# Two output tiles per weight unit, and two PSUM banks in turn, in the output projection of a decoder step

## The reference

```
h      = rms_norm(x, norm_g)
z      = h @ w_in                      # feeds four branches and the merge gates
y_n    = branch_n(z)                   # retention, gated delta, short convolution, pooling; width 512 each
merged = sum_n sigmoid(gate_n) * (y_n @ w_branch[n])
x      = x + merged @ w_out            # the output projection, 2048 x 2048
```

## Time and profile before

| what | value |
|---|---|
| three runs | 2049.70, 2051.76, 2053.64 us (median 2051.76) |
| profiled execution, first to last instruction | 2049.6 us |
| PE busy / weight loads busy | 1992.3 / 1976.0 us |
| DVE busy | 1346.1 us |
| ACT busy | 1113.6 us |
| POOL busy | 186.5 us |
| mean granted TensorE clock | 0.993 |

### The profile page before, as it was taken

The page is one execution under the profiler, slowest core; times in us unless marked ns, Lnnn a source line. Parts: engine busy times, 40 slices in busy tenths (PEclk is TensorE's granted clock), DMA queues, the critical chain, the costliest instruction groups (busy, mean ns, idle before and its releaser), DMA issues.

```text
span 2049.6 us, 50596 instructions
## 1 busy us (share of the span) xinstructions
PE 1992.3 (97%) x16294; PEld 1976.0 (96%) x16294; DVE 1346.1 (66%) x2608; ACT 1113.6 (54%) x2045; POOL 186.5 (9%) x345
## 2 busy tenths in 40 slices
PE   6999999999999999999999999999999999999996
PEld 6999999999999999999999999999999999999996
DVE  7887566755656556666678766676565656566666
ACT  5556556645455555555555655655464645455554
POOL 2111110110101010000011210001010100100000
PEclk9999999999999999999999999999999999999998
DMA  6655555555554545665656555655555555566664
GB/s 209 190 175 172 157 181 162 184 160 156 154 172 135 176 140 167 188 180 180 184 172 184 171 173 155 190 164 175 165 162 160 162 155 149 160 175 179 178 184 161
DMA packets 183252, 348.13 MB, mean 170 GB/s; under 512 B 20592, under 2 KB 20720, under 8 KB 182992
## 3 DMA queue, kind: packets, MB, share of 16 engines
q1 hardware_dynamic: 177552, 326.45, 53.4%
q0 software_dynamic: 5568, 19.80, 3.0%
HBM read 333.61 MB, written 12.56 MB: 169 GB/s over the span
## 4 chain that ended last, share of the span: by engine, by line
PE 90%; DVE 4%; issue 3%; ACT 2%; DMA 1%; DVEq 0%; ACTq 0%; SPq 0%
PE acc L1301 27%; PE acc L1302 27%; PE acc L1303 26%; DMA raw<-w_stream 1%; PE side L1514 1%; PE side L1488 1%; DVE wlo L829 1%; PE side L1512 1%; PE side L1505 1%; ACT whi L540 1%; PE side L1396 1%; PE side L1495 1%; PE side L1402 1%; PE side L1358 1%; DVE act_lo L841 0%
## 5 line engine op out<-in xcount | busy, mean ns | idle before, releaser
L829 DVE TENSOR_TENSOR wlo<-raw,whi 128x512 fp32r<-128x512 f32 x1219 | 828.3, 694 | 488.4 <-ACT whi L540 481.4
L540 ACT ACTIVATE whi<-raw 128x512 fp32r<-128x512 f32 x1219 | 751.5, 628 | 643.7 <-PE acc L1303 553.9
L1301 PE MATMUL acc<-act_hi,whi 128*128 128x264 f32 x3328 | 972.6, 292 | 40.1 <-issue 19.6
L1303 PE MATMUL acc<-act_hi,wlo 128*128 128x264 f32 x3328 | 947.8, 285 | 0.0
L1302 PE MATMUL acc<-act_lo,whi 128*128 128x264 f32 x3328 | 947.2, 285 | 0.0
L1301 PEld LDWEIGHTS acc<-act_hi,whi 128*128 128x128 f32 x3328 | 631.8, 190 | 48.2 <-issue 35.9
L1302 PEld LDWEIGHTS acc<-act_lo,whi 128*128 128x128 f32 x3328 | 632.8, 190 | 0.9
L1303 PEld LDWEIGHTS acc<-act_hi,wlo 128*128 128x128 f32 x3328 | 629.4, 189 | 0.0
L1301 PE MATMUL acc<-y_hi,whi 128*128 128x264 f32 x1536 | 439.9, 286 | 0.0
L1302 PE MATMUL acc<-y_lo,whi 128*128 128x264 f32 x1536 | 435.4, 283 | 0.0
L1303 PE MATMUL acc<-y_hi,wlo 128*128 128x264 f32 x1536 | 434.8, 283 | 0.0
(11 more groups left out here) (267 smaller groups left out, 1438.2 us busy)
## 6 DMA issues: line engine op xcount, KB each, us to landing
raw<-w_stream SPq DMA_DIRECT2D x1220, 256.0 KB, 2.8
state<-ret_in POOLq DMA_DIRECT2D x8, 512.0 KB, 5.5
s_ret<-state POOLq DMA_DIRECT2D x8, 512.0 KB, 4.6
state<-gdn_in POOLq DMA_DIRECT2D x8, 512.0 KB, 5.4
s_gdn<-state POOLq DMA_DIRECT2D x8, 512.0 KB, 6.1
x<-x_in SPq DMA_DIRECT2D x4, 528.0 KB, 6.5
y_out<-wide SPq DMA_DIRECT2D x4, 396.0 KB, 2.8
con<-consts SPq DMA_DIRECT2D x1, 1582.0 KB, 11.8
```

What stands on the lines that cost most here:

```text
L540: sc.activation(whi[:, s, :], raw[:, s, :], ACT.Copy).then_inc(hi_ready, 1)
L829: ve.tensor_tensor(wlo[:, s, :], raw[:, s, :], whi[:, s, :].bitcast(F32), ALU.subtract).then_inc(lo_ready, 1)
L1301: mm(acc[bank][:, 0:N], w_h, hi[:, k0 + k, :], start=first and k == 0, stop=False)
L1303: op = mm(acc[bank][:, 0:N], w_l, hi[:, k0 + k, :], start=False, stop=last and k == UK - 1)
```

## The change

A unit of the output projection now holds two k-tiles of two neighbouring output tiles instead of four k-tiles of one. PE takes a pair of output tiles through eight units. Within a unit every matmul writes the other bank than the one ahead of it. The pair is finished at once, so DVE and ACT handle two tiles together, every eight units. Stream length, unit size and the number of matmuls are unchanged. The last turn of the ACT and DVE loops is written out after the loop.

```diff
-                with pe.Fori(0, BT) as h:
-                    unit = streamer(l, OFF_O, h, TURN)
-                    blocks(unit, 0, TURN, pe.snap(l * BANK_USES + BK_O + h), y_hi, y_lo, ready=mlo_ready)
+                def pair(ub, j, bank, k0, first, last):
+
+                    pe.wait_ge(lo_ready, ub + j + 1 + RING)
+                    s = j % RING
+                    for k in range(2):
+                        cols = [slice((2 * k + b) * P, (2 * k + b + 1) * P) for b in range(2)]
+                        for b in range(2):
+                            mm(acc[bank + b][:, 0:N], whi[:, s, cols[b]], y_hi[:, k0 + k, :], start=first and k == 0, stop=False)
+                        for b in range(2):
+                            mm(acc[bank + b][:, 0:N], whi[:, s, cols[b]], y_lo[:, k0 + k, :], start=False, stop=False)
+                        for b in range(2):
+                            op = mm(acc[bank + b][:, 0:N], wlo[:, s, cols[b]], y_hi[:, k0 + k, :], start=False,
+                                    stop=last and k == 1)
+                    op.then_inc(unit_used, 1)
+
+                with pe.Fori(0, BT) as h:
+                    ub = pe.snap(l * UNITS + OFF_O + h * TURN)
+                    free = pe.snap(l * BANK_USES + BK_O + h)
+                    for i in (0, 2):
+                        pe.wait_ge(bank_free[i], free + BF)
+                        pe.wait_ge(bank_free[i + 1], free + BF)
+                        for u in range(2 * UB):
+                            if i == 0:
+                                pe.wait_ge(mlo_ready, l * UB * UK + 2 * (u + 1))
+                            pair(ub, i * UB + u, i, 2 * u, u == 0, u == 2 * UB - 1)
```

DVE (ACT follows the same order, with its square and `act_hi` where DVE has `x_added` and `x_lo`, and waits for `x_updated` of each tile there):

```diff
-                with dve.Fori(0, BT) as h:
+                def out_turn(h, last):
                     ub, split = splitter(l, OFF_O, h, TURN)
-                    for i in range(4):
-                        split(4 * i + 3, 4 * i + 7)
-                        k = dve.snap(h * 4 + i)
-                        dve.wait_ge(unit_used, ub + RING + UB * (i + 1))
-                        ve.tensor_tensor(tile_of(x, k), tile_of(x, k), acc[i][:, 0:N], ALU.add).then_inc(bank_free[i], 1)
-                        dve.wait_ge(bank_free[i], l * BANK_USES + BK_O + h + 1 + BF)
-                        dve.sem_inc(x_updated, 1)
-                        x_added(i % 2, l * KT + h * 4 + i)
-                        x_lo(l + 1, k, (l + 1) * KT + h * 4 + i)
+                    for a in (0, 8):
+                        split(a + 5, a + 11)
+                        dve.wait_ge(unit_used, ub + RING + a + 2 * UB)
+                        for t in (a // 4, a // 4 + 1):
+                            k = dve.snap(h * 4 + t)
+                            ve.tensor_tensor(tile_of(x, k), tile_of(x, k), acc[t][:, 0:N], ALU.add).then_inc(bank_free[t], 1)
+                            dve.wait_ge(bank_free[t], l * BANK_USES + BK_O + h + 1 + BF)
+                            dve.sem_inc(x_updated, 1)
+                        for i in range(2):
+                            if not (last and a):
+                                split(a + 11 + i, a + 12 + i)
+                            t = a // 4 + i
+                            x_added(t % 2, l * KT + h * 4 + t)
+                            x_lo(l + 1, dve.snap(h * 4 + t), (l + 1) * KT + h * 4 + t)
+
+                ub, split = splitter(l, OFF_O, 0, TURN)
+                split(3, 5)
+                with dve.Fori(0, BT - 1) as h:
+                    out_turn(h, False)
+                out_turn(BT - 1, True)
...
-    for m in range(KT):
-        parts += [units(w_out, m * P)]
+    for m in range(0, KT, 2):
+        two = w_out[:, :, m * P:(m + 2) * P].reshape(DEPTH, KT // 2, 2, P, 2 * P)
+        parts += [two.transpose(0, 1, 3, 2, 4).reshape(DEPTH, KT // 2, P, UC)]
```

More of the change, by code:

```diff
@@ L801, in _ @@
                     merged_hi(k)
-                with act.Fori(0, BT) as h:
+                def out_turn(h, last):
                     ub, split = splitter(l, OFF_O, h, TURN)
-                    for i in range(4):
-                        split(4 * i + 3, 4 * i + 7)
[L808 to L811, removed]
+                    for a in (0, 8):
[4 more added lines that the diff above has]
+                            t = a // 4 + i
+                            k = act.snap(h * 4 + t)
+                            act.wait_ge(x_updated, l * KT + h * 4 + t + 1)
+                            x_square(k, t % 2, l * KT + h * 4 + t)
+                            x_hi(l + 1, k)
+                ub, split = splitter(l, OFF_O, 0, TURN)
+                split(3, 5)
+                with act.Fori(0, BT - 1) as h:
+                    out_turn(h, False)
+                out_turn(BT - 1, True)
             for k in range(FINAL_DVE, KT):
```

## The result

| | before | after |
|---|---|---|
| median of 20 runs each | 2051.61 us | 2054.59 us |
| profiled execution, first to last instruction | 2049.6 us | 2053.6 us |
| first projection, first to last matmul start | 92.68 us | 93.90 us |
| second projection | 92.68 us | 93.90 us |

The ratio is 1.0015, 95% interval 1.0009 to 1.0021: 3.1 us slower (1.8 to 4.3). The forecast was 2053.4, with a range of 2048.5 to 2059.

The account below looks back on a forecast made before the run. The prediction took the distance between PE's matmul starts to bound the projections. It added 0 for the loop, 0.65 us for the first layer's end and 0.93 for the kernel's end: +1.6, 2053.4 us, range 2048.5 to 2059.

Parts of the forecast that it names:

- PE's matmul distance bounds the stage; DVE, ACT and the transfers hide.: Output projections: the distance between matmul starts sets the stage; work of the other engines and transfers adds 0 within the loop.
- the 2.1 us that the prediction named: Slack expected in the loop between DVE's split of unit 11's weights after a pair and PE's need for them.
- A bank change costs 0.: Output projections: switching PSUM bank at every matmul costs nothing, argued from 15 bank changes in the old projection.
- Hence the distance stays 0.12083.: Both projections: 1536 matmul distances stay at 0.12083 us each, adding 0 to the time.
- its own sign ("I am wrong if the distance is not 0.1208"): Stated test of failure: a projection matmul distance other than 0.1208 us, or PE waiting for `wlo` within the stage.
- its first rival, a cost of bank changes: Projections: each bank change costs up to 8 ns, giving 2065.7 us; it decides from 1.6 ns a matmul; chance 0.10.
- The bounds (-7.7 to +12.3 us): Both projections: possible effect of bank changes, -5 to +8 ns per matmul times 1536; 0 was taken.
- Nothing of the 10.8 ns above 264 columns at 2.4 GHz belongs to the bank.: Projection matmuls: the 10.8 ns beyond 0.1100 us is no same-bank penalty; the rival that it is had chance 0.07.
- Added waits on PE are free.: Projection turns: 8 waits on `mlo_ready` instead of 4, all already met, cost 0.
- End of the first layer, +0.65 us.: After the first layer's last matmul, ACT's handling of two tiles delays PE's fourth unit of the second layer by 0.65 us.
- The end, +0.93 us.: After the kernel's last matmul, DVE's second sum comes 0.94 us later, so the square root starts 0.93 us later.
- The clock stays.: Projections: PE stays at 2.4 GHz; the rival of a falling clock gave 2130 us, chance 0.02.

Follow-up runs that it names:

- e1: Changed kernel, but both tiles of a pair accumulate in one bank, so no bank change at every matmul: first projection 93.90 us.
- e3: Changed kernel with old units and old order of weights and activations, evacuation in pairs, banks written in turn by every matmul: first projection 92.68 us.
- e4: Changed kernel with old units, old order and one bank for 48 matmuls, keeping evacuation in pairs: projection 92.68 us, whole 1.0004 of the kernel before.
- e5: Changed kernel's units, but per k-tile three matmuls of one output tile, then three of the other: projection 93.90 us, whole 1.0026 of the kernel before.
- e6: Changed kernel with the y_hi and y_lo tiles padded to 272 columns apart instead of 264: projection 93.12 us.
- e7: Changed kernel, but every projection matmul reads the first tile of y_hi or y_lo (products not the reference's): projection 92.04 us.
- e2: Changed kernel's units, but six matmuls of one output tile, then six of the other, k-tiles in old order: projection 92.58 us, whole 1.0007 of the kernel before.
- e10: Changed kernel reading tiles 0 and 8, then 1, then 4 within each turn: tile 4's units took 1480 or 1481 ns in turns one and three, 1440 or 1441 otherwise.

## Why the prediction was right, and where its steps were off

- *PE's matmul distance bounds the stage; DVE, ACT and the transfers hide.* Right: PE waits for nothing in either projection, after as before. ACT's two waits for a transfer (2.8 us together) did not reach PE: the split of every unit was done 0.8 us or more before PE began it, and from the sixth unit on the 2.1 us that the prediction named.
- *A bank change costs 0.* Right, and now shown: e1 against the changed kernel and e3 against e4 change nothing but the banks, and the lengths agree to 1 ns. The argument from 15 changes of bank in the old projection held. (The stage ahead of it has 31, not 30.)
- *Hence the distance stays 0.12083.* This step failed. The sum took 0 for 1536 distances; they cost 1.6 ns more each, 2 x 1.22 = 2.44 us, more than the whole +1.6 us forecast. The prediction looked at what changes from matmul to matmul in the result (the bank) and took the order of what is read as free. e5 against e4 shows it in its place: six matmuls on a tile index instead of three. By its own sign ("I am wrong if the distance is not 0.1208") the prediction was wrong here, and 1.6 ns is just what it named as deciding for its first rival, a cost of bank changes, which is false. That the time came close is in part luck: the two edges, put too high, made up for a part of it. The bounds (-7.7 to +12.3 us) held the term, but for another reason than named: the extra 16 ns of a block of 60 in the stage ahead were taken for a possible cost of bank changes; e6 shows that they come from where the y tiles lie.
- *Nothing of the 10.8 ns above 264 columns at 2.4 GHz belongs to the bank.* Right by e1 and e3. The least over a whole projection is 120.00 ns, with one tile in e7; single units of e2 take 1433 ns, 119.4 a distance. What the rest above 110.0 is made of is open.
- *Added waits on PE are free.* Right: e2 has all of them, and its 92.58 us are below those of before. In the changed kernel the first eight units of a turn have the waits on `mlo_ready` and the second eight have none, with the same lengths.
- *End of the first layer, +0.65 us.* Right that ACT's table load sets the fourth unit, but mis-sized: +0.10 to +0.17 in four traces without a fall of the clock, +0.7 and +0.85 in two. The prediction counted the 2.64 us of idle time as fixed and let `act_hi` or the last wait push it; it was 2.00 to 2.98 with `act_hi` always at the same place. The stall ahead of the fourth unit was to grow from 0.30 to 0.95; it was 0.26 to 0.49 in the four, 1.2 and 1.3 in the two, and none where the clock fell.
- *The end, +0.93 us.* Right mechanism, 0.67 us measured. DVE's second sum comes 0.71 later than the one sum of before, not 0.94. The first sum starts at e+1.28 instead of 1.33, and the first `act_lo` only 0.35 behind it, where the prediction took the 0.53 of before; the second sum follows that by 0.40, as forecast. Where the clock fell around PE's sum, 0.4 to 0.55 us come on top.
- *The clock stays.* Right in the projections (1.00), in all runs, with banks in turn or not. The rule of the Trainium skill (TensorE: Matmul & The Clock Gate, A second HAM failure mode: psum-queue depth-cycling) that work cycling through banks can lose the clock did not show there. The clock fell behind the gap between the layers, in half of all traces, at a price of about 1.2 us that the sum has no term for.

Sum by what was measured: 2.44 + 0.15 + 0.67 = 3.3 us, against 3.1 (1.8 to 4.3) in the timed runs and 1.6 in the forecast. The 0.15 and the 0.67 are the lower values that the traces show for the edges; with the upper ones (0.85 and 1.22) it would be 4.5, so only the 2.44 is firm. That e4 (edges alone) is at 1.0004 and the changed kernel at 1.0015 leaves 0.0011, that is 2.3 us, for the order, near the 2.44 of the traces; the intervals of the two overlap.

**What stays open:** why the distance depends on the order of the activation tiles. Shown is what it does not depend on (bank, weight blocks, hi or lo, evacuation) and what moves it (the sequence of tile indices, the distance of tiles in memory, and something that differs from turn to turn in e10). No kernel here that gives the reference's result was shown faster than the kernel before: e2's projection is 0.10 us shorter than the old one, less than its edges cost.

## What to carry to other kernels

Where TensorE is the bound, read the distance between matmul starts, not its busy share, and compare it over a whole stage: 1.6 ns in 120 is 1.2 us in 768 matmuls and shows in no wait. To argue that a reordering is free, list everything that its order changes for each matmul (output bank, weight block, moving tile), and find a row for each; here a row had been looked for only for the bank. When a rival's threshold is met, test its mechanism before believing it: 1.6 ns a matmul looked like the cost of a bank change until one run took the bank changes away. Work handled in pairs is paid at the end of a stage, where the second item follows the first with nothing beside it.

## What the runs showed of the hardware that was not expected

- The distance between matmuls of 264 columns at 2.4 GHz with a weight load each was 120.00 to 122.43 ns on average over a projection, by the sequence of activation tiles (119.4 in one unit of e2, 123.4 in one of e10); the whole projection agreed within 2 ns between the layers in every run.
- Moving the y tiles from 1056 to 1088 bytes apart took 0.78 us off a projection (e6) and 16 ns off the one unit of each block of the stage ahead that reads them (1465 to 1449), with the same instructions.
- The same instructions on the same tile took 1440 ns in one turn and 1480 in the next (e10).
- Writing two PSUM banks in turn changed nothing: 93.902 us with and 93.902 us without (e1), 92.680 with (e3) and 92.680 without (before).
